# Deferring the first norm of a two-block layer kernel, and moving its depthwise convolution and low weight parts between engines

## What is computed

```python
h = rmsnorm(x, mix_pre_norm)                    # x * rsqrt(mean(x*x) + eps) * gain
u = h @ w_in                                     # 1024 x 3072: u_a, u_b, hq, hk, hv, hg, 512 columns each
y_conv = silu(layernorm(conv31(u_a * sigmoid(u_b)) + dw_b))       # depthwise, 31 taps, causal
q, k = rotary(hq), rotary(hk) * 128 ** -0.5      # 4 heads of 128
o = chunkwise_retention(q, k, hv); o = o * rsqrt(mean(o*o) + eps) # per head
x = x + rmsnorm(concat([y_conv, silu(hg) * o]) @ w_out, mix_post_norm)
mem_n = rmsnorm(mem, mem_norm)                   # the second block's memory, 256 x 1024
keys  = mem_n @ w_mem_kv[:, :512]                # made in the first block's stage
```

## Time and profile before

| what | value |
|---|---|
| median of 3 runs | 909.87 us (909.6 to 910.76) |
| the profiled execution: its time | 910.12 us |
| its span (first to last instruction) | 908.3 us |
| PE, PEld busy | 894.9 us (99%), 784.3 us (86%) |
| DVE, ACT, POOL busy | 617.7 us (68%), 503.8 us (55%), 310.8 us (34%) |
| chain that ended last | PE 91%, DVE 3%, ACT 2%, DMA 2% |
| HBM read | 161.40 MB, 179 GB/s over the span |

### The profile page before, as it was taken

The page is one execution under the profiler, slowest core; times in us unless marked ns, Lnnn a source line. Parts: engine busy times, 40 slices in busy tenths (PEclk is TensorE's granted clock), DMA queues, the critical chain, the costliest instruction groups (busy, mean ns, idle before and its releaser), DMA issues.

```text
span 908.3 us, 15484 instructions
## 1 busy us (share of the span) xinstructions
PE 894.9 (99%) x6436; PEld 784.3 (86%) x6436; DVE 617.7 (68%) x767; ACT 503.8 (55%) x732; POOL 310.8 (34%) x118
## 2 busy tenths in 40 slices
PE   8999999999999999999999999999999999999997
PEld 6998986888888878999999998877788788888886
DVE  4986747888884256757798766663324689999623
ACT  6543747444454356755656575555545566666533
POOL 4000001666664410000000007646783166666542
PEclk9999999999999999999999999999999999999999
DMA  9693463555555544545535334544454365555551
GB/s 354 225 295 107 151 232 136 212 186 185 188 189 211 199 146 180 186 158 194 206 142 187 141 101 159 183 144 156 163 194 156 132 232 193 191 194 194 183 188 47
DMA packets 32295, 163.95 MB, mean 180 GB/s; under 512 B 9154, under 2 KB 11602, under 8 KB 13794
## 3 DMA queue, kind: packets, MB, share of 16 engines
q1 hardware_dynamic: 32018, 162.62, 52.1%
q10 hardware_dynamic: 144, 0.26, 0.1%
q0 software_dynamic: 64, 0.08, 0.0%
HBM read 161.40 MB, written 1.57 MB: 179 GB/s over the span
## 4 chain that ended last, share of the span: by engine, by line
PE 91%; DVE 3%; ACT 2%; DMA 2%; POOL 1%; issue 1%; SPq 1%; DVEq 0%; ACTq 0%
PE ring L1738 19%; PE acc L1873 17%; PE ring L2227 12%; PE ring L1772 9%; PE acc L1772 9%; PE ring L1819 6%; PE ring L1776 5%; PE acc L1776 4%; DMA raw<-wstream 2%; PE acc L1925 1%; DVE w_lo L1160 1%; PE acc L2082 1%; PE acc L1886 1%; ACT w_hi L724 1%; PE ring L1849 1%; PE ring L1757 1%
## 5 line engine op out<-in xcount | busy, mean ns | idle before, releaser
L724 ACT CAST w_hi<-raw 128x1024 fp32r<-128x1024 f32 x284 | 297.0, 1052 | 316.3 <-PE ring L1738 78.4
L671 POOL TENSOR_TENSOR w_lo<-raw,w_hi 128x1024 fp32r<-128x1024 f32 x101 | 290.4, 2878 | 352.2 <-ACT w_hi L724 352.0
L1160 DVE TENSOR_TENSOR w_lo<-raw,w_hi 128x1024 fp32r<-128x1024 f32 x183 | 236.5, 1303 | 122.8 <-ACT w_hi L724 113.4
L1738 PE MATMUL ring<-h,w_hi 128*128 128x256 f32 x960 | 174.4, 284 | 1.3 <-issue 1.0
L1738 PEld LDWEIGHTS ring<-h,w_hi 128*128 128x128 f32 x960 | 149.7, 192 | 1.5 <-issue 1.3
L1738 PE MATMUL ring<-h,w_lo 128*128 128x256 f32 x480 | 135.8, 283 | 0.0
L1738 PEld LDWEIGHTS ring<-h,w_lo 128*128 128x128 f32 x480 | 92.1, 192 | 1.0 <-issue 1.0
L1873 PE MATMUL acc<-w_hi,ff 128*128 128x512 f32 x340 | 91.1, 390 | 0.0
L1772 PE MATMUL ring<-h,w_hi 128*128 128x512 f32 x352 | 88.1, 392 | 0.0
L1772 PE MATMUL acc<-h,w_hi 128*128 128x512 f32 x336 | 84.6, 394 | 0.0
L695 POOL TENSOR_SCALAR_AFFINE_SELECT toep_t<-toep_t 64x2304 f32<-64x2304 f32 x2 | 5.7, 2848 | 224.3 <-DMA toep_t<-toep 224.1
(11 more groups left out here) (291 smaller groups left out, 1359.5 us busy)
## 6 DMA issues: line engine op xcount, KB each, us to landing
raw<-wstream SPq DMA_DIRECT2D x142, 1024.0 KB, 4.9
u<-uconv SPq DMA_DIRECT2D x4, 426.0 KB, 9.8
toep_t<-toep SPq DMA_DIRECT2D x16, 96.0 KB, 3.2
x<-x_tok SPq DMA_DIRECT2D x2, 512.0 KB, 5.2
mem<-mem_tok SPq DMA_DIRECT2D x1, 1024.0 KB, 11.1
w_ple<-wproj SPq DMA_DIRECT2D x1, 1024.0 KB, 7.1
decay<-decay_tab SPq DMA_DIRECT2D x1, 768.0 KB, 6.5
out_t<-y SPq DMA_DIRECT2D x3, 256.0 KB, 2.1
```

The costliest lines, as they stand in the source:

```text
L671: nc.gpsimd.tensor_tensor(w_lo[:, u % UNITS], unit_of_raw(u), as_f32(w_hi[:, u % UNITS]), ALU.subtract).then_inc(lo_ready["pool"], 1)
L724: nc.scalar.copy(w_hi[:, u % UNITS], unit_of_raw(u)).then_inc(hi_ready, 1)
L1160: V.tensor_tensor(w_lo[:, u % UNITS], unit_of_raw(u), as_f32(w_hi[:, u % UNITS]), ALU.subtract).then_inc(lo_ready["dve"], 1)
L1738: last = mm(dst, w[a], src[:, b, kt], start=n == 0 and i == 0, stop=n == kts - 1 and i == 2)
```

## The change

1. **First norm deferred.** x comes a second time, by channel (`x_ch` into `y`, first in the SP queue), with a small table `pre` of the two gains by channel. `h` is x times the gain (split over ACT 4, DVE 2, POOL 2 tiles; low parts on DVE, `first_lo`), without the root: no transposes ahead of the products. `unnormed_pair` makes `conv` 0 in the order hi\*hi, hi\*lo for both units, then lo\*hi. The root is computed beside it; PE spreads it along rows (`row_spread`) after unit 3, DVE copies it to `r_row`, and it is applied later: to every `conv` fill and every `g` fill by a DVE product in PSUM (`row_scaled`), to the rotary table (for q and k), and to v as ACT's scale (`v_out`).
2. **Convolution.** `PACKED` is tile 3 alone; DVE makes tiles 0, 1, 2 with all sums but the last in PSUM (`sc[j]`), 93 taps where there were 31.
3. **Low weights.** POOL makes them for units 6 to 21, DVE no longer does; POOL's `w_conv` is one product behind unit 17.
4. **Memory norm.** Its squares move on ACT behind the `conv` gates, its normed copy from DVE to ACT (without gain), and the gain goes into the splits, as four instructions of 128x128 each on ACT and DVE in place of one of 128x512.
5. The loads of params, mem and token x are later in the SP queue; one mem key tile is cut so that the spread of the retention root stands in its middle.

```diff
-PACKED = (1, 2, 3)
+PACKED = (3,)
+XT_ACT, XT_DVE = 4, 6
-    ("first_x", 0, 4, 0, "dve"), ("conv", 0, 4, 16, "dve"), ("qk", 0, 4, 16, "act"),
+    ("conv", 0, 4, 16, "dve"), ("qk", 0, 4, 16, "act"),
+TAPS_FROM, TAPS_TO = 6, FIRST_BLOCK[INDEX[("g", 1)]] // UB
 def _lo_engine(u):
-    if u == 0 or _within(u, _POOL_ONLY):
+    if _within(u, _POOL_ONLY) or TAPS_FROM <= u < TAPS_TO:
         return "pool"
...
+            sp.dma_start(y[:], x_ch).then_inc(load_xt, 16)
+            sp.dma_start(pre_col[:], pre).then_inc(load_pre, 16)
+            sp.dma_start(raw[:, 0, 0:UB], wstream[0][:, 0:UB]).then_inc(first_unit_ready, 16)
+            sp.dma_start(raw[:, 0, UB:], wstream[0][:, UB:]).then_inc(slot_ready[0], 16)
```

On ACT:

```diff
+            act.wait_ge(load_xt, 16)
+            for k in range(XT_ACT):
+                A(h[:, 0, k], y[:, k], ACT.Identity, scale=pre_col[:, k:k + 1]).then_inc(xt_hi_act, 1)
...
+            for j in range(4):
+                wait_fill("conv", j)
+                act.wait_ge(conv_scaled, j + 1)
+                wait_gate_slot(act, "conv", j)
+                A(gate_tmp[:, gate_slot("conv", j), 0], bank("conv", j)[:, 1], ACT.Sigmoid).then_inc(gate_done, 1)
             act.wait_ge(load_mem, 16)
             for tt in range(2):
                 mean_square("mem", tt, mem[:, tt], q_tok[:, tt])
                 deviation("mem", tt)
-            act.wait_ge(load_params, 32)
-
-            for j in range(4):
-                wait_fill("conv", j)
-                wait_gate_slot(act, "conv", j)
-                A(gate_tmp[:, gate_slot("conv", j), 0], bank("conv", j)[:, 1], ACT.Sigmoid).then_inc(gate_done, 1)
             act.wait_ge(lb_exp, 1)
             A(lb[:, 1], lb[:, 0], ACT.Exp).then_inc(lb_exp, 1)
             for j in range(2):
                 copy_fill("qk", j, q_raw[:, 2 * j:2 * j + 2])
```

On DVE (what is left out is the memory's norm, and then the mean's copy and subtraction):

```diff
+            feed(TAPS_FROM)
+            dve.wait_ge(row_spread, 1)
+            V.tensor_copy(r_row[:], st[:, 0:S]).then_inc(row_ready, 1)
...
             for j in range(4):
                 gates[0] += 1
-                feed_behind("conv", j)
+                row_scaled("conv", j, conv_scaled)
+                if j:
+                    taps(4)
                 wait_gate(gates[0])
                 V.tensor_tensor(conv_in[:, j, CW - 1:CW - 1 + S], bank("conv", j)[:, 0], gate_tmp[:, gate_slot("conv", j), 0],
                                 ALU.mult).then_inc(freed["dve"], 1)
...
                 wait_read(dve, "conv", j)
                 tiles_in[0] = j + 1
-                taps(4)
+                taps((6, 10, 10, 0)[j])
...
-            for j in range(4):
-                feed_behind("qk", j)
-                taps(4)
+            taps(24)
+            for tt in range(2):
+                n = NORM["mem", tt]
+                dve.wait_ge(dev_ready, n + 1)
+                V.reciprocal(sums[:, 2, n:n + 1], sums[:, 1, n:n + 1]).then_inc(mem_inverse, 1)
+            taps(CW * (4 - len(PACKED)))
             dve.wait_ge(load_side, 48)
+            after(link(V.tensor_tensor(rope[:], rope[:], over(r_row[:], 2), ALU.mult)))
             rope_of(0, q_raw)
+            turned_lo("mem", 0)
+            turned_lo("mem", 1)
...
             rope_of(1, k_raw)
```

On PE:

```diff
+            for _ in range(12):
+                mm(sc[2][:, 0:P], rstd[:, 0:P], rstd[:, 0:P], start=True, stop=True)
+            pe.wait_ge(load_xt, 16)
+            for _ in range(8):
+                mm(sc[2][:, 0:P], rstd[:, 0:P], rstd[:, 0:P], start=True, stop=True)
+            unnormed_pair("conv")
+            pair("conv", 1, h)
+            pe.wait_ge(load_ident, 16)
+            pe.wait_ge(load_params, 32)
+            pe.wait_ge(pre_inverse, 2)
+            for tt in range(2):
+                n = NORM["mix_pre", tt]
+                last = mm(st[:, tt * P:tt * P + P], sums[:, 2, n:n + 1].to_broadcast([P, P]), mat("ident"),
+                          start=True, stop=True)
+            last.then_inc(row_spread, 1)
+            for j in range(2, 4):
+                pair("conv", j, h)
```

More of the change, by code:

```diff
@@ L180 @@
 SUMS = ("wout", "down", "ple", "wout2", "down2")
-NORMED = ("first", "mem", "wout", "ple", "wout2")
-TURNS = ("first", "mem", "wout", "down", "ple", "merged", "wout2")
+NORMED = ("mem", "wout", "ple", "wout2")
+TURNS = ("mem", "wout", "down", "ple", "merged", "wout2")
 HALVED = ("wout2", "down2")
@@ L338, in program @@
         mix_keys = sem("mix_keys")
-        load_x = [sem(f"load_x{i}") for i in range(2)]
+        load_x = sem("load_x")
         load_ident = sem("load_ident")
@@ L769, in turned_hi @@
                 act.wait_ge(t_turned, 4 * TURNS.index(stage) + k + 1)
+                if stage == "mem":
+                    for i in range(4):
+                        kt = 4 * (k % 2) + i
+                        ins = A(turned_h(stage, k, 0)[:, i], turned_bank(stage, k)[:, i], ACT.Identity,
+                                scale=pre_col[:, KT + kt:KT + kt + 1])
+                    ins.then_inc(t_hi, 1)
+                    return
                 nc.scalar.copy(turned_h(stage, k, 0), turned_bank(stage, k)).then_inc(t_hi, 1)
@@ L1236, in turned_lo @@
                 dve.wait_ge(t_hi, 4 * TURNS.index(stage) + k + 1)
+                if stage == "mem":
+                    for i in range(4):
+                        kt = 4 * (k % 2) + i
+                        ins = V.scalar_tensor_tensor(out=turned_h(stage, k, 1)[:, i], in0=turned_bank(stage, k)[:, i],
+                                                     scalar=pre_col[:, KT + kt:KT + kt + 1],
+                                                     in1=as_f32(turned_h(stage, k, 0)[:, i]),
+                                                     op0=ALU.mult, op1=ALU.subtract)
+                    ins.then_inc(freed["dve"], 1)
+                    return
                 V.tensor_tensor(turned_h(stage, k, 1), turned_bank(stage, k), as_f32(turned_h(stage, k, 0)),
@@ L1286, in taps, with row_scaled @@
                         tap(min(left, key=lambda j: (tap_of[j], j)))
+            feed(TAPS_FROM)
+            dve.wait_ge(row_spread, 1)
+            V.tensor_copy(r_row[:], st[:, 0:S]).then_inc(row_ready, 1)
+            dve.wait_ge(row_ready, 1)
+            def row_scaled(name, j, signal):
+                dve.wait_ge(pe_step, fill_step(fi(name, j)))
+                V.tensor_tensor(bank(name, j), bank(name, j), over(r_row[:], 2), ALU.mult).then_inc(signal, 1)
             dve.wait_ge(pad_ready, 1)
@@ L1978, in _ @@
             last.then_inc(ret_spread, 1)
-            pair("memk", 1, mem_n)
+            tile_out(fill[:, 1], mem_n)
             def wout_ready(i, tt):
```

192 lines of the change are left out of this document (131 added, 61 removed).

## The result

| | before | after |
|---|---|---|
| median | 910.32 us (909.6 to 912.29) | **924.24 us** (921.85 to 925.05) |
| profiled execution: time, span | 910.12, 908.3 us | 924.56, 922.6 us |
| PE busy | 894.9 us (99%) | 893.1 us (97%) |
| DVE, ACT, POOL busy | 617.7, 503.8, 310.8 us | 635.0, 508.4, 344.0 us |

After to before: 1.0143, interval 1.0124 to 1.0162. The change makes the kernel 1.4% slower; 920.0 us was forecast, and 924.2 lies inside the range of 911 to 927. TensorE's busy time is nearly that of before, though 7 us of packed convolution are gone.

A forecast was written before the change was run, and what follows sets the result against it. The prediction took TensorE's queue, 99% busy, as the bound. Gains of 9.2 us against waits of 19.0, less 1.0 for existing gaps, gave +8.8; with 1.4 for the clock, 920.3 profiled and 920.0 us median, range 911 to 927.

The forecast's parts named there:

- Start, -2.5: Kernel start: earlier loads and no transposes bring the third weight unit at 16.35 us instead of 18.86, 2.5 us earlier.
- the walk: The prediction's hand timing of four instruction streams from row durations, each instruction starting when engine and waits allow.
- Packing and spread: TensorE's convolution packing takes 3.5 us instead of 10.57 (7.05 less); spreading the root along rows adds 0.35.
- Waits at the fills: Convolution stage: late gates and casts make TensorE wait 0.9 us at unit 6, 1.0 at unit 10, 7.5 at unit 12.
- Rotations held, 9.2: Before the mean's copy: GpSimd holds four of five VectorE instructions, 9.2 us in sum; copy at 86.5 us.
- Last mem transpose 103.2 after 4.3 us: Behind the mean: VectorE's serial chain and ScalarE's table load delay this transpose from 97.92 to 103.2, TensorE waiting 4.3 us.
- Units 20 and 24, 1.3 and 2.2: TensorE waits 1.3 us at unit 20 with GpSimd held, and 2.2 up to unit 24 behind a serial mem chain.
- Squares: Ahead of wout: squares of the retention output come 1.8 us late behind casts, gate and table load.
- Clock, 1.4: After the 7.5 and 4.3 us waits TensorE runs at half pace, costing 1.4 us (bounds nothing and 2.9).
- What lies behind 116.97 us: From wout's first product to the end: 791.3 us of span, claimed unchanged.
- The rival of gains kept: Convolution stage: scaling and taps keep pace, nothing waits, 9.2 us are gained, giving 900.7 us; chance 0.10.
- the rival of held taps: Taps summed in PSUM are still held by GpSimd's low parts, some 20 us more, 940 us; chance 0.09 (or worse).

The follow-up runs named there:

- e1_banks: The changed kernel with each projection after the first norm back on its earlier PSUM bank (index + 1, modulo 3): 918.03 us.
- e7_gates_first: e1_banks with no convolution tap before the last gate, all 93 taps following the gates on VectorE: 911.05 us.
- e6_pack3: e1_banks with TensorE packing three convolution tiles again instead of one: 925.81 us.
- e12: e1_banks with only nine taps before the last gate, second rotation and lb ahead of mem's splits, g's scaling ahead of the root, one tile packed: 910.53 us.
- e9_sbuf: e1_banks with the taps' running sums in SBUF instead of PSUM: 939.42 us.

## Why the prediction was right, and where it was not

The direction and its mechanism hold: what the two edits give is taken back by waits for VectorE's and ScalarE's work. The size was right in part by luck. The forecast had 10.2 us lost up to wout, the clock's 1.4 with it, and nothing behind; measured are 7.55 and 6.75. An error of 2.7 one way took back part of one of 6.75 the other way.

- **Start, -2.5: measured -4.6.** The step was mis-sized. x was in use from 5.82 us and the first half slot of weights from 7.63, where the walk had 7.1 and 8.6. Part of that is arithmetic: the slices of rows 3, at the share that the prediction names, give 6.5 and 8.2. The first product came at 8.40 for 9.7, and the microsecond of waiting for low parts behind it was 0.1 (14.26 - 8.40 is 5.86, and 48 products of 0.12 are 5.76). The gain does not outlive the conv stage: the last scaling is at 44.13 us, 0.4 ahead of the forecast 44.5.
- **Packing and spread:** 3.66 us for 3.5, and 0.6 for 0.35.
- **Waits at the fills:** 7.32 for 7.5 at unit 12; 1.5 for 0.9 at unit 6; 1.1 for 1.0 at unit 10. Four chained taps in PSUM take 1.96 us (28.74 to 30.70), 0.49 each as in SBUF; over nine the average is 0.51 (31.74 to 36.34), since the next instruction starts before the last tap has ended, and that weighs less among nine. ScalarE does what the walk said:

```profile
44.86 0.39 ACT L875 ACTIVATE gate_tmp<-ring 128x256 f32<-128x256 f32 x1 [5.53 <-DVE ring L1382]
...
50.56 0.21 ACT L881 ACTIVATE lb<-lb 128x16 f32<-128x16 f32 x1
50.69 1.97 ACT L748 CAST w_hi<-raw 128x1024 fp32r<-128x1024 f32 x2
```

- **Rotations held, 9.2:** the table's product and the first rotation lost 7.8 us (2.17, 3.32 and 6.67 where 0.69, 1.22 and 2.47 are their own). Copy of the mean 87.1 for 86.5, but not for this reason: VectorE had 3.03 us to spare ahead of it, so the copy would not have come sooner without the holding. The walk had made 1.1 us of it; by the trace it is nothing. It is the wait at unit 12, through TensorE and ScalarE, that brings the copy so late.
- **Last mem transpose 103.2 after 4.3 us:** 102.29 after 2.8. What failed here is "ScalarE loads its table and passes it on": the table was loaded long before, while ScalarE waited.

```profile
94.25 1.28 ACT L906 ACT_TABLE_LOAD   x1
101.64 0.60 ACT L906 ACTIVATE g_ret<-ring 128x512 f32<-128x512 f32 x1 [6.11 <-DVE ring L1382]
```

- **Units 20 and 24, 1.3 and 2.2:** no such waits. Squares 1.5 for 1.8. Wout 124.5 for 125.7, 7.55 us late where the sum said 8.8.
- **Clock, 1.4:** this term stands as 1.6 us behind the wait at unit 12 (half pace from 54.3 to 57.5) and 1.5 behind that at 102.3 (to 105.3). Neither was removed by itself. By the chain of the profile the first lies on the way to the copy of the mean and the second beside it, as ScalarE and VectorE carry the chain from 101 to 114 us. Together they are more than the 1.4 and than the upper bound of one unit (2.9), and behind the 3.6 us wait, where it could be isolated, stand 3.0 more.
- **"What lies behind 116.97 us is 791.3 us of span which the change leaves as it is": it is 798.1.** This is the step that failed: the term behind wout was put at nothing, and it is 6.75 us. e1_banks shows it as the shift of banks (791.6 with the old banks). The four entries that left the list are in the diff, and the list decides the bank of all later ones; I followed them only as far as wout.
- **The rival of gains kept** named the pitch of the taps, together with the place of mem's squares, as its point. e7_gates_first and e6_pack3 show another that comes first: that the taps stand ahead of the gates. Only with that mended do the taps' number and pitch count, and then they do: with 93 of them TensorE waits 4.5 us (e7) and 6.9 us (e12) for VectorE. No order tried reached the rival's 900.7. e9_sbuf shows the rival of held taps to be real for the other choice of operand, at 21 us where I had priced 20.

## What to carry to other kernels

When a change takes an entry from a list whose index picks a buffer, compare who frees each buffer before and after, to the end of the program: here that alone cost 6 us, 450 us behind the edit. On an engine that runs its instructions in order put first what other engines wait for (a gate, a split that frees a bank) and filler work such as taps last; the same instructions in another order made 918.0, 911.1 or, with one tile more packed, 904.8 us. Two marks that stay a constant distance apart over many variants (37.4 us from the copy to wout here) name a serial chain between them: moving anything ahead of the first is worth nothing of that distance. And look for the idle time just ahead of a mark before calling the work in front of it the bound: VectorE's held rotations lost 7.8 us and moved nothing.
